# A hybrid decoder step on one core: the x tiles normed one by one, the next x and the first output stage's inputs brought forward, a sample's small work and stores moved

## The chip, the core and the metric

The kernel runs on one core of a Trainium2 chip. The metric is the device time of one execution in microseconds (us). A core has five engines with a queue of instructions each: TensorE (PE), VectorE (DVE), ScalarE (ACT), GpSimd (POOL) and SyncE (SP). They run in parallel and wait for each other through semaphores; inside one engine everything runs in the order written. Transfers are issued by SP, ACT and POOL and moved by 16 shared DMA engines.

## What is computed

One layer over 2048 prompt rows and 8 x 4 sample rows of width 1024, all in float32:

```
h = rms_norm(x, g_mix_pre)
z = h @ w_in                                   # 1024 -> 2048, split into 8 groups of 256
y_a = pool_mixer(z[:256])                      # trailing means over 2, 4, 8, 16 rows
y_b = conformer_conv(z[256:768])               # GLU, 31 taps, head LayerNorm, swish
y_c, v = chunk_spatial_gating(z[768:1280])     # head LayerNorm of v, lower-triangular 128x128
y_d = short_gated_conv(z[1280:])               # 3 taps
o = concat(y_a, y_b, y_c, y_d) @ w_out
x = x + rms_norm(o, g_mix_post)
f = square(relu(rms_norm(x, g_ffn_pre) @ w_up)) @ w_down
x = x + rms_norm(f, g_ffn_post)
```

It returns the new x of both kinds of rows, the last 15, 30 and 2 rows of three mixers' inputs (the states) for prompt and samples, and the samples' normed v.

## The kernel before, in words

**Matmuls.** Each float32 operand is split into a high and a low part. `split_hi` (ACT) writes `w_hi` from a weight panel in `raw`, `split_lo` (DVE) writes `w_lo = raw - w_hi`. PE's `three` (L1695 to L1697) multiplies hi by hi, hi by lo and lo by hi. A panel is 1024 x 256 weights (1 MB). `raw`, `w_hi` and `w_lo` have two slots each, and panel j uses slot j % 2.

**Order of the work.** The 2048 rows go in four blocks b of 512. The list `order` names the panels: first the eight input panels of each block (kind "I", called GATE, PV, AV, CV, HV, BV, UV, VV), then the four output panels of block 0 (kind "O"), then for each block the panels of the feed-forward part ("U" and "D"), with the O panels of the next block between the D panels. J2 = 32 is the first O panel. Each engine's program walks this list with code of its own. What an engine does between the panels is written out by hand, so the order of the calls in the program is the order of the work.

**Before panel 0.** SP loads four x tiles of block 0 (128 rows each) and then weight panels 0 and 1. ACT's `x_stat(b)` squares and sums the four tiles and takes one square root for all four; DVE's `x_norm(b)` takes one reciprocal and scales the four tiles. PE's `transpose_x` turns a tile into columns in the banks `tr[0]` and `tr[1]`, ACT's `h_hi(n)` and DVE's `h_lo(n)` write the two parts into `act_hi` and `act_lo`. PE transposes small parameter rows and the gating weights ahead of the first x tile, and the sample rows and a bias product behind the last one, all ahead of panel 0.

**Between two blocks.** The x tiles of block b + 1 are loaded into `raw`, which only blocks 1 to 3 leave free: their split weights come from scratch in HBM. For block 1 the loads wait until `raw` is done with the last two panels of block 0. `x_stat(b + 1)` and `x_norm(b + 1)` stand inside block b; PE transposes the tiles between the four 128-row chunks of the last panel, VV, because `act_hi` and `act_lo` have one slot. DVE spreads the 31 taps of the convolution (`taps`, L1122) over block b and the start of the next.

**The sample's small work.** In block 2, after the UV panel, ACT issues 24 small stores of sample states, then squares and roots the sample's v (L820, L822), for which DVE waits inside `sample_v` (L1278), and issues one more store.

**The first output stage.** `mix_in` (POOL) loads a tile of the four mixers' results from scratch into `mixc`, and `mix_part` (ACT, then DVE) splits it. DVE's `o_copy` moves a finished bank to `o_sb`, ACT's `o_squares` sums its squares. Between the copies stand the last block's leftovers: `v_centre`, `v_sum`, `v_scale` (LayerNorm of v), `centre`, `gate`, `conv_scale`, `conv_out`. PE's `gating_of`, `mean_of` and `var_of` serve them between the panels. After the fourth panel `f_of_first` norms the rows for the feed-forward part and PE transposes them (L1921).

Of the kernel before, what the change touches and what calls it, by code (L numbers as in the profile page):

```python
# [5 lines left out]
def hybrid_trunk_step(nc, x_prompt, x_sample, state_pool, state_conv, state_short, g_mix_pre, g_mix_post,  # L6
# [71 lines left out]
    bank_of, wrote, freed = {}, [0] * NRING, [0] * NRING  # L78
# [19 lines left out]
    with ctx:  # L98
# [37 lines left out]


# [24 lines left out]
        ch_ext = sb("ch_ext", [P, 2, HS + N1], to=p1)  # L162
        b_raw = sb("b_raw", [P, 2, N1], to=p1)
        c_short = sb("c_short", [P, 2, N1], to=p1)
        a_ext = sb("a_ext", [P, 2, HP + N1], to=p1)
# [233 lines left out]
        def x_tile(n):  # L399

            r = n % NCH
            if n < NCH:
# [45 lines left out]
        def _(sp):  # L448
            for i in range(NCH):
                sp.dma_start(x_tile(i), x_prompt[0, i * P:(i + 1) * P, :]).then_inc(x_full[i], 16)  # L450
            sp.dma_start(x_smp[:, :], x_sample.rearrange("b t c -> (b t) c")).then_inc(xsmp_full, 16)
# [12 lines left out]
            for j, (kind, b, q, p) in enumerate(order):  # L464
                s = j % 2
                if j not in part_no:
# [4 lines left out]
                    sp.dma_start(raw[:, s, :, :], source(j)).then_inc(raw_full[s], 16)  # L471
                    raw_user[s] = j
                if j == NI - 1:
                    for r in range(2):
                        sp.wait_ge(lo_ready, split_no[NI - 2 + r])
                        x_in_raw(1, r)
                if kind == "I" and p == 2 and 0 < b < NB - 1:
                    for s in range(2):
                        sp.wait_ge(x_tr, 2 * NCH * (b + 1))
                        x_in_raw(b + 1, s)  # L480
                if kind == "I" and p == 4 and b == 0:
# [13 lines left out]
        def _(pool):  # L495
# [77 lines left out]
            for j in part_no:  # L573
# [13 lines left out]
                if p == 7:  # L587
                    store(b, 0, ya_done, pool_d[:, :, :])
            store(NB - 1, 3, yd_done, c_short[:, :, :])

# [3 lines left out]
            pool.wait_ge(nst_tr, 2)  # L594
            pool.wait_ge(mix_st[0], MIX_ST)
            for i in range(2):
                mix_in(0, i)
            for g, dst in ((g_mix_post, g_mix), (g_ffn_pre, g_up), (g_ffn_post, g_out)):
                pool.dma_start(dst[:, :], g[0].partition_broadcast(P)).then_inc(s_gains, 16)
            for i in range(2):  # L600
                rows_in("x", 0, i)
# [24 lines left out]
        def _(act):  # L626
# [10 lines left out]
            def x_stat(b):  # L637
                for i in range(NCH):
                    act.wait_ge(x_full[i], 16 * (b + 1))
                    act.wait_ge(x_sq, NCH * b + i)  # L640
                    if b == 1 and i == 0:
                        act.wait_ge(smp_step, 1)
                    SC.activation(junk[:, :], x_tile(NCH * b + i), ACT.Square, accum_out=xms[:, i:i + 1])\
# [1410 lines left out]
```

## Time and profile before

| | |
|---|---|
| median of 3 runs | 2289.42 us (2289.16 to 2293.85) |
| the profiled execution's own time | 2289.91 us |
| its span, first to last instruction | 2288.1 us |
| PE busy | 2147.0 us, 94% of the span |
| PE weight load busy | 1945.0 us, 85% |
| DVE busy | 1081.4 us, 47% |
| ACT busy | 752.6 us, 33% |
| mean granted TensorE clock | 0.977 |

The clock is a share of 2.4 GHz; it has two levels, 0.5 (1.2 GHz) and 1.0. In a timeline row the bracket at the end holds the time that the engine stood idle just before, and who ended it. Times in rows count from the start of the span.

### The profile page before, as it was taken

The numbers are of one execution on the slowest core, as the hardware profiler recorded it, in microseconds if no ns is written. First come the engines' busy times: TensorE is split into PE (matmuls) and PEld (weight loads), VectorE is DVE, ScalarE is ACT, GpSimd is POOL, SyncE is SP. The second block draws the span as 40 slices with busy tenths as digits, with TensorE's granted clock in tenths as the row PEclk, the third lists the DMA queues.
The fourth block names the chain that finished last, engine by engine and source line by source line (L and its number), as shares of the span: only waits on it lengthen the run. The fifth ranks groups of instructions, "written<-read, shape, count | busy, mean of one in ns | idle before, by whom it ended". The sixth has DMA issues, their size and how long they took to land.

```text
span 2288.1 us, 32980 instructions
## 1 busy us (share of the span) xinstructions
PE 2147.0 (94%) x14425; PEld 1945.0 (85%) x14425; DVE 1081.4 (47%) x1388; ACT 752.6 (33%) x1145; POOL 115.0 (5%) x205
## 2 busy tenths in 40 slices
PE   6989997979699999999999999999999989999996
PEld 4877775768488988988898899889898989999996
DVE  3677766775643333465333346533334553334243
ACT  4233232224333223443323244332324442313131
POOL 2000110010000000000000000000000000000000
PEclk9999998989799999999999999999999999999998
DMA  6754644553232223445233334533223434222221
GB/s 211 242 212 170 212 169 170 180 192 103 102 112 93 93 93 102 131 154 166 93 99 99 98 130 148 166 100 102 93 93 119 137 115 135 85 83 78 90 74 60
DMA packets 186084, 291.87 MB, mean 128 GB/s; under 512 B 6128, under 2 KB 162453, under 8 KB 177733
## 3 DMA queue, kind: packets, MB, share of 16 engines
q1 hardware_dynamic: 160997, 168.64, 23.2%
q0 software_dynamic: 24656, 120.96, 15.0%
q8 instruction: 114, 1.87, 0.3%
q14 instruction: 30, 0.24, 0.0%
q10 hardware_dynamic: 287, 0.16, 0.0%
HBM read 247.24 MB, written 42.80 MB: 127 GB/s over the span
## 4 chain that ended last, share of the span: by engine, by line
PE 66%; issue 18%; DVE 7%; ACT 4%; DMA 3%; ACTq 0%; POOL 0%; SPq 0%; POOLq 0%; DVEq 0%
PE mm L1695 21%; PE mm L1696 21%; PE mm L1697 21%; ACT w_hi L635 2%; DVE w_lo L1079 2%; DVE conv L1122 2%; DMA mixc<-mixT_scratch 1%; DMA x_in<-in_x_prompt 1%; PE tr L1700 1%; PE tr L1729 1%; DMA raw<-in_w_in 1%; PE tr L1921 0%; DVE o_sb L1399 0%; PE mm L1756 0%; DVE conv_s L1606 0%
## 5 line engine op out<-in xcount | busy, mean ns | idle before, releaser
L1079 DVE TENSOR_TENSOR w_lo<-raw,w_hi 128x2048 fp32r<-128x2048 f32 x152 | 348.4, 2292 | 707.1 <-ACT w_hi L635 707.1
L1695 PE MATMUL mm<-act_hi,w_hi 128*128 128x512 f32 (+1 forms) x1728 | 638.5, 369 | 9.8 <-DVE act_lo L1417 6.0
L1696 PE MATMUL mm<-act_lo,w_hi 128*128 128x512 f32 (+1 forms) x1728 | 632.6, 366 | 0.0
L1697 PE MATMUL mm<-act_hi,w_lo 128*128 128x512 f32 (+1 forms) x1728 | 630.0, 365 | 0.0
L1695 PE MATMUL mm<-w_hi,u_hi 128*128 128x256 f32 (+1 forms) x2176 | 603.3, 277 | 1.5
L1697 PE MATMUL mm<-w_hi,u_lo 128*128 128x256 f32 (+1 forms) x2176 | 601.0, 276 | 0.0
L1696 PE MATMUL mm<-w_lo,u_hi 128*128 128x256 f32 (+1 forms) x2176 | 600.9, 276 | 0.0
L635 ACT ACTIVATE w_hi<-raw 128x2048 fp32r<-128x2048 f32 x152 | 290.8, 1913 | 582.0 <-PE mm L1697 581.1
L1695 PEld LDWEIGHTS mm<-w_hi,u_hi 128*128 128x128 f32 (+1 forms) x2176 | 398.3, 183 | 4.8 <-DVE u_lo L1433 3.6
L1696 PEld LDWEIGHTS mm<-w_lo,u_hi 128*128 128x128 f32 (+1 forms) x2176 | 398.3, 183 | 1.2
L1697 PEld LDWEIGHTS mm<-w_hi,u_lo 128*128 128x128 f32 (+1 forms) x2176 | 398.3, 183 | 0.7
L1695 PEld LDWEIGHTS mm<-act_hi,w_hi 128*128 128x128 f32 x1728 | 327.4, 189 | 68.8 <-issue 13.4
L1697 PEld LDWEIGHTS mm<-act_hi,w_lo 128*128 128x128 f32 x1728 | 327.1, 189 | 56.3
L1696 PEld LDWEIGHTS mm<-act_lo,w_hi 128*128 128x128 f32 x1728 | 327.1, 189 | 55.2 <-issue 2.4
L1695 PE MATMUL mm<-w_hi,act_hi 128*128 128x256 f32 (+1 forms) x736 | 210.3, 286 | 17.7 <-DVE act_lo L1365 14.9
L1697 PE MATMUL mm<-w_hi,act_lo 128*128 128x256 f32 (+1 forms) x736 | 208.2, 283 | 0.0
L1696 PE MATMUL mm<-w_lo,act_hi 128*128 128x256 f32 (+1 forms) x736 | 208.0, 283 | 0.0
L904 ACT ACTIVATE square<-mm 128x512 f32<-128x512 f32 (+1 forms) x160 | 81.8, 511 | 262.5 <-PE mm L1697 262.5
L1122 DVE SCALAR_TENSOR_TENSOR conv<-g_ext,cst,conv 128x512 f32<-128x512 f32 x240 | 162.6, 745 | 0.7 <-ACT conv L739 0.7
L1695 PEld LDWEIGHTS mm<-w_hi,act_hi 128*128 128x128 f32 (+1 forms) x736 | 133.7, 182 | 20.2 <-issue 15.5
L1431 DVE CAST u_hi<-square 128x512 fp32r<-128x512 f32 (+1 forms) x160 | 59.9, 374 | 192.3 <-ACT square L906 192.3
L1696 PEld LDWEIGHTS mm<-w_lo,act_hi 128*128 128x128 f32 (+1 forms) x736 | 133.3, 181 | 2.2 <-issue 0.5
(238 smaller groups left out, 1350.4 us busy)
## 6 DMA issues: line engine op xcount, KB each, us to landing
raw<-in_w_ffn_up SPq DMA_DIRECT2D x64, 1024.0 KB, 5.4
raw<-in_w_ffn_down SPq DMA_DIRECT2D x64, 1024.0 KB, 5.1
w_hi<-whi_scratch POOLq DMA_DIRECT2D x24, 1024.0 KB, 5.2
w_lo<-wlo_scratch POOLq DMA_DIRECT2D x24, 1024.0 KB, 7.9
raw<-in_w_out SPq DMA_DIRECT2D x16, 1024.0 KB, 5.3
raw<-in_w_in SPq DMA_DIRECT2D x8, 1024.0 KB, 9.5
whi_scratch<-w_hi POOLq DMA_DIRECT2D x8, 1024.0 KB, 8.7
wlo_scratch<-w_lo POOLq DMA_DIRECT2D x8, 1024.0 KB, 10.7
```

The lines of the kernel that those rows point to most:

```text
L635: SC.activation(w_hi[:, s, :, :], raw[:, s, :, :], ACT.Copy).then_inc(hi_ready, 1)
L904: SC.activation(square[:, at % 2, 0:c1 - c0], mm[bank][:, 0:c1 - c0], ACT.Relu).then_inc(bank_free[bank], 1)
L1079: DVE.tensor_tensor(w_lo[:, s, :, :], raw[:, s, :, :], w_hi[:, s, :, :].bitcast(fp32), ALU.subtract)\
L1122: DVE.scalar_tensor_tensor(out=c, in0=g_ext[:, t, k:k + N1], scalar=col("conv_w", 2 * k + t), in1=c, op0=ALU.mult, op1=ALU.add).then_inc(c ...
L1431: DVE.tensor_copy(u_hi[:, k, c0:c1], square[:, at % 2, 0:c1 - c0]).then_inc(u_hi_ready, 1)
L1695: PE.matmul(out, whi, xhi, start=(k == 0), stop=False)
L1696: PE.matmul(out, whi, xlo, start=False, stop=False)
L1697: return PE.matmul(out, wlo, xhi, start=False, stop=(k == K - 1))
L1700: PE.matmul(bank[:, 0:n], headmean[:, :], src, start=True, stop=True).then_inc(done, 1)
L1729: last = PE.transpose(tr[hh][:, kk * P:(kk + 1) * P], x_tile(n)[:, k * P:(k + 1) * P], ident[:, :])
```

## The change

1. **Start.** Panel 0's weights are loaded from ACT's queue as its first instruction, and panel 1's from SP ahead of the small rows. One square root on a one-column tile `warm` stands before the first x. `x_stat` and `x_norm` take one tile at a time (one root and one reciprocal each) and are interleaved with `h_hi`, `h_lo` and the split of panel 0. PE's small transposes and the bias product become `small_parts`, called after the first half of panel 0.
2. **Next x.** The four x tiles of block 1 go to `v_n` and to three tiles of `x0`, loaded from j = 3 on. Their `x_stat` stands after `split_hi(5)`. The tiles of block 2 go to `raw` without waiting for the transposes of block 1.
3. **Sample's v and small stores.** `sample_v` is cut into three parts that stand between taps at the start of block 2; the 25 sample stores and the 3 prompt state stores are issued by SP.
4. **First output stage.** The last block's state transposes (`last_rows`) stand after the first half of UV. `split_lo(J2)` stands three taps later, the first `mix_part` six taps later; `v_centre` and what follows it come behind all four `mix_part`. `mix_in(0, 0)` no longer waits for the last store of the pool mixer. `gating_of`, `mean_of` and `var_of` come one panel later.
5. **Ring.** The first output stage uses four PSUM banks, the rest six in turn.

```diff
-            bank = len(bank_of) % NRING
+            bank = turn % 4 if j < J2 + NP else (turn - 2 * NP + 4) % NRING
...
-            if n < NCH:
+            if n == NCH:
+                return v_n[:, :, :].rearrange("p a c -> p (a c)")
+            if n < 2 * NCH:
                 return x0[:, r, :]
...
+            sp.dma_start(raw[:, 1, :, :], source(1)).then_inc(raw_full[1], 16)
...
+                if j == 3:
+                    sp.wait_ge(bias_ready, 1)
+                    for r in range(NCH):
+                        sp.wait_ge(x_tr, 2 * NCH)
+                        sp.dma_start(x_tile(NCH + r), x_prompt[0, N1 + r * P:N1 + (r + 1) * P, :])\
+                          .then_inc(x_full[r], 16)
...
+            act.dma_start(raw[:, 0, :, :], source(0)).then_inc(raw_full[0], 16)
             act.wait_ge(pool_init, 5)
+            SC.activation(warm[:, :], eps[:, :], ACT.Sqrt)
...
             b = NB - 1
-            v_centre(b)
-            for i in range(2):
-                mix_part(0, i)
-            split_lo(J2 + 1)
-            v_sum(b)
-            for i in range(2, NCH):
-                mix_part(0, i)
-            v_scale(b)
-            token_panel(J2, o_copy)
+            mix_part(0, 0)
+            mix_part(0, 1)
+            taps(b, range(28, 30))
+            mix_part(0, 2)
+            taps(b, range(30, 31))
+            mix_part(0, 3)
+            split_lo(J2 + 1)
+            v_centre(b)
+            v_sum(b)
+            token_panel(J2, o_copy)
+            v_scale(b)
+            token_panel(J2 + 1, o_copy)
             centre(b)
             gate(b)
-            token_panel(J2 + 1, o_copy)
-            conv_scale(b)
             token_panel(J2 + 2, o_copy)
+            conv_scale(b)
             conv_out(b)
             last_o_panel(J2 + 3)
```

ACT in the same stage:

```diff
-            v_square(b)
-            for i in range(2):
+            for i in range(NCH):
                 mix_part(0, i)
             split_hi(J2 + 1)
-            for i in range(2, NCH):
-                mix_part(0, i)
+            v_square(b)
             v_root(b)
             token_panel(J2, o_squares)
+            token_panel(J2 + 1, o_squares)
             conv_square(b)
-            token_panel(J2 + 1, o_squares)
             conv_root(b)
             token_panel(J2 + 2, o_squares)
```

How the instructions stand on an engine, before and now:

ACT at the very start, before:

```order
L643 ACT_TABLE_LOAD
L643 ACTIVATE junk,xms<-x 128x1024 x4
L647 ACT_TABLE_LOAD
L647 ACTIVATE xroot<-xms,eps 128x4
L699 ACTIVATE cst<-tr 128x78
L701 ACTIVATE sgu_wT<-tr 128x512
L635 ACTIVATE w_hi<-raw 128x2048
L706 ACTIVATE junk,sms<-x_smp 32x1024
L708 ACTIVATE sms<-sms,eps 32x1
L653 ACTIVATE act_hi<-tr 128x4x128 x8
```

ACT at the very start, now (as far as the second tile's high part):

```order
L730 DMA raw<-in_w_in 128x8x256
L732 ACT_TABLE_LOAD
L732 ACTIVATE warm<-eps 128x1
L675 ACTIVATE junk,xms<-x 128x1024
L679 ACTIVATE xroot<-xms,eps 128x1
L675 ACTIVATE junk,xms<-x 128x1024
L679 ACTIVATE xroot<-xms,eps 128x1
L686 ACTIVATE act_hi<-tr 128x4x128 x2
L675 ACTIVATE junk,xms<-x 128x1024
L679 ACTIVATE xroot<-xms,eps 128x1
L666 ACTIVATE w_hi<-raw 128x2048
L686 ACTIVATE act_hi<-tr 128x4x128 x2
```

The one table load between the squares and the root is gone, the high part of the first tile stands ahead of the split of panel 0's weights, and the third tile's statistics stand between them.

DVE where the first output stage begins, before (the taps are `conv<-g_ext,cst,conv`, two instructions each):

```order
L1079 TENSOR_TENSOR w_lo<-raw,w_hi 128x2048
L1122 SCALAR_TENSOR_TENSOR conv<-g_ext,cst,conv 128x512 x24
L1135 TENSOR_REDUCE v_small<-v_raw 128x16
L1137 TENSOR_SCALAR v_small<-v_small 128x16
L1140 TENSOR_TENSOR v_n<-v_raw,v_small 128x1024
L1365 TENSOR_TENSOR act_lo<-mixc,act_hi 128x8x128 x2
L1079 TENSOR_TENSOR w_lo<-raw,w_hi 128x2048
```

DVE at the same place, now:

```order
L1155 SCALAR_TENSOR_TENSOR conv<-g_ext,cst,conv 128x512 x6
L1111 TENSOR_TENSOR w_lo<-raw,w_hi 128x2048
L1155 SCALAR_TENSOR_TENSOR conv<-g_ext,cst,conv 128x512 x12
L1416 TENSOR_TENSOR act_lo<-mixc,act_hi 128x8x128 x2
L1155 SCALAR_TENSOR_TENSOR conv<-g_ext,cst,conv 128x512 x4
L1416 TENSOR_TENSOR act_lo<-mixc,act_hi 128x8x128
L1155 SCALAR_TENSOR_TENSOR conv<-g_ext,cst,conv 128x512 x2
L1416 TENSOR_TENSOR act_lo<-mixc,act_hi 128x8x128
L1111 TENSOR_TENSOR w_lo<-raw,w_hi 128x2048
L1168 TENSOR_REDUCE v_small<-v_raw 128x16
```

Twelve taps' instructions and `v_centre` stood between the weights and the first `mix_part` and no longer do.

DVE at the end of the first output stage, before (from the copies of the second panel to those of the fourth):

```order
L1378 COPY o_sb<-mm 128x2x256
L1165 RECIPROCAL inv_c<-inv_c 128x512 x2
L1168 TENSOR_TENSOR conv<-conv,inv_c 128x512 x2
L1378 COPY o_sb<-mm 128x2x256
L1079 TENSOR_TENSOR w_lo<-raw,w_hi 128x2048
L1378 COPY o_sb<-mm 128x2x256
L1174 TENSOR_TENSOR conv<-sqcv,inv_c 128x512 x2
L1378 COPY o_sb<-mm 128x2x256 x2
```

DVE at the same place, now (from `gate` to the copies of the fourth panel):

```order
L1219 TENSOR_TENSOR u_sb<-v_raw,u_sb 128x512 x2
L1429 COPY o_sb<-mm 128x2x256
L1111 TENSOR_TENSOR w_lo<-raw,w_hi 128x2048
L1429 COPY o_sb<-mm 128x2x256
L1198 RECIPROCAL inv_c<-inv_c 128x512 x2
L1201 TENSOR_TENSOR conv<-conv,inv_c 128x512 x2
L1207 TENSOR_TENSOR conv<-sqcv,inv_c 128x512 x2
L1429 COPY o_sb<-mm 128x2x256 x2
```

The reciprocals stood ahead of the third panel's copies and its weight split, and now stand behind them, directly ahead of `conv_out`.

## Rows read from the trace of the kernel before

**Rows 1.** The page's first part: busy time of each engine.

```profile
PE 2147.0 (94%) x14425; PEld 1945.0 (85%) x14425; DVE 1081.4 (47%) x1388; ACT 752.6 (33%) x1145; POOL 115.0 (5%) x205
```

**Rows 2.** Waits of PE: who waited for whom, us in total, times, longest.

```profile
PE tr L1729 <- DVE act_lo L1111: 29.2, 6, 14.0
PE tr L1921 <- DVE f_sb L1409: 20.9, 5, 15.6
```

**Rows 3.** Timeline of the start: start us, us, engine, instruction, [idle before].

```profile
12.04 1.06 ACT L643 ACTIVATE junk<-x 128x1024 bf16<-128x1024 f32 x1 [1.73 <-DMA x<-in_x_prompt]
13.21 1.28 ACT L647 ACT_TABLE_LOAD   x1
...
18.36 1.91 ACT L635 ACTIVATE w_hi<-raw 128x2048 fp32r<-128x2048 f32 x1 [0.93 <-DMA raw<-in_w_in]
...
31.14 0.69 DVE L1111 TENSOR_TENSOR act_lo<-tr,act_hi 128x512 fp32r<-128x512 f32 x1 [0.16 <-ACT act_hi L653]
...
33.13 0.80 PE L1695 MATMUL mm<-act_hi,w_hi 128*128 128x512 f32 x1
...
46.80 0.28 PE L1695 MATMUL mm<-w_hi,act_hi 128*32 128x256 f32 x1
```

**Rows 4.** Timeline at the end of block 0, DVE and PE.

```profile
135.46 0.18 DVE L1099 RECIPROCAL xinv<-xroot 128x4 f32<-128x4 f32 x1 [5.84 <-ACT xroot L647]
135.67 4.88 DVE L1104 SCALAR_TENSOR_TENSOR raw<-raw,xinv,gpre 128x1024 f32<-128x1024 f32 x4
...
151.77 1.94 PE L1729 MATMUL tr<-ident,raw 128*128 128x128 f32 x8 [6.94 <-DVE act_lo L1111]
```

**Rows 5.** Timeline at the end of block 2, DVE and PE.

```profile
354.48 0.41 DVE L1275 TENSOR_TENSOR vs_n<-zs,vs_small 32x256 f32<-32x256 f32 x1
...
372.44 0.41 DVE L1278 TENSOR_REDUCE vs_small<-vs_out 32x4 f32<-32x256 f32 x1 [17.54 <-ACT vs_out L820]
...
386.78 1.94 PE L1729 MATMUL tr<-ident,raw 128*128 128x128 f32 x8 [14.00 <-DVE act_lo L1111]
```

**Rows 6.** Windows, PE alone: us, busy (instructions), granted clock, DMA share, GB/s.

```profile
151.80:157.70 5.90, 5.90 (x28) 0.50 0.00 0
386.80:391.90 5.10, 5.10 (x32) 0.69 0.01 3
545.20:567.50 22.30, 22.30 (x192) 1.00 0.28 85
```

**Rows 7.** Timeline where the first output stage begins.

```profile
489.23 2.29 DVE L1079 TENSOR_TENSOR w_lo<-raw,w_hi 128x2048 fp32r<-128x2048 f32 x1 [10.53 <-ACT w_hi L635]
491.44 15.98 DVE L1122 SCALAR_TENSOR_TENSOR conv<-g_ext,cst,conv 128x512 f32<-128x512 f32 x24
507.35 1.21 DVE L1135 TENSOR_REDUCE v_small<-v_raw 128x16 f32<-128x1024 f32 x1
...
513.46 0.55 PE L1695 MATMUL mm<-w_hi,act_hi 128*128 128x256 f32 x1 [14.87 <-DVE act_lo L1365]
...
519.14 1.06 ACT L855 ACTIVATE act_hi<-mixc 128x1024 fp32r<-128x1024 f32 x1 [4.33 <-DMA mixc<-mixT_scratch]
...
527.68 2.57 PE L1756 MATMUL mm<-sgu_wT,v_n 128*64 128x128 f32 x32
...
531.60 0.68 PE L1695 MATMUL mm<-w_hi,act_hi 128*128 128x256 f32 x1
```

**Rows 8.** Timeline where the first output stage ends.

```profile
545.44 2.29 DVE L1079 TENSOR_TENSOR w_lo<-raw,w_hi 128x2048 fp32r<-128x2048 f32 x1 [6.91 <-ACT w_hi L635]
...
550.03 6.57 DVE L1165 RECIPROCAL inv_c<-inv_c 128x512 f32<-128x512 f32 x2 [1.70 <-ACT inv_c L685]
...
568.09 0.69 DVE L1174 TENSOR_TENSOR conv<-sqcv,inv_c 128x512 f32<-128x512 f32 x1 [3.94 <-ACT inv_c L693]
...
570.11 1.28 DVE L1378 COPY o_sb<-mm 128x512 f32<-128x512 f32 x2
...
583.11 1.97 PE L1921 MATMUL tr<-ident,f_sb 128*128 128x128 f32 x8 [15.58 <-DVE f_sb L1409]
```

More of the change, by code:

```diff
@@ L702, in _ @@
               .then_inc(init_copied, 1)
-            split_hi(0)
-            act.wait_ge(xsmp_full, 16)
-            act.wait_ge(x_sq, NCH)
-            SC.activation(junk[0:NS, :], x_smp[:, :], ACT.Square, accum_out=sms[:, 0:1]).then_inc(smp_step, 1)
-            act.wait_ge(smp_step, 1)
-            SC.activation(sms[:, 1:2], sms[:, 0:1], ACT.Sqrt, bias=eps[0:NS, :], scale=1.0 / D).then_inc(smp_step, 1)
-            for n in range(NCH):
-                h_hi(n)
-            split_hi(1)
             act.wait_ge(smp_tr, 1)
@@ L758, in _ @@
                     split_hi(5)
+                    for i in range(NCH):
+                        x_stat(NCH + i)
                 if b == 1:
@@ L1289, in _ @@
             x_norm(0)
+            x_norm(1)
+            h_lo(0)
+            x_norm(2)
             split_lo(0)
-            for n in range(NCH):
-                if n == 1:
-                    dve.wait_ge(smp_step, 2)
-                    DVE.reciprocal(sms[:, 2:3], sms[:, 1:2]).then_inc(smp_step, 1)
-                    dve.wait_ge(smp_step, 3)
-                    DVE.scalar_tensor_tensor(out=x_smp[:, :], in0=x_smp[:, :], scalar=sms[:, 2:3], in1=gpre[0:NS, :],
-                                             op0=ALU.mult, op1=ALU.mult).then_inc(smp_step, 1)
-                h_lo(n)
+            h_lo(1)
+            x_norm(3)
+            h_lo(2)
+            h_lo(3)
+            dve.wait_ge(smp_step, 2)
+            DVE.reciprocal(sms[:, 2:3], sms[:, 1:2]).then_inc(smp_step, 1)
+            dve.wait_ge(smp_step, 3)
+            DVE.scalar_tensor_tensor(out=x_smp[:, :], in0=x_smp[:, :], scalar=sms[:, 2:3], in1=gpre[0:NS, :],
+                                     op0=ALU.mult, op1=ALU.mult).then_inc(smp_step, 1)
+            split_lo(1)
             dve.wait_ge(smp_hi, 1)
@@ L1301, in _ @@
                               act_hi[:, :, N1:NX].bitcast(fp32), ALU.subtract).then_inc(smp_lo, 1)
-            split_lo(1)
             dve.wait_ge(init_tr, 3)
@@ L1345, in _ @@
                 if b < NB - 1:
-                    x_norm(b + 1)
-                if b == 2:
-                    sample_v()
+                    for i in range(NCH):
+                        x_norm(NCH * (b + 1) + i)
                 taps(b, range(15, 19))
@@ L1351, in _ @@
                 if last:
+                    taps(b, range(19, 22))
                     split_lo(J2)
-                    taps(b, range(19, 31))
+                    taps(b, range(22, 28))
                 else:
@@ L1708, in _ @@
             pe.wait_ge(pool_init, 8)
-            pe.wait_ge(s_rows, 16 * len(ROWS))
-            PE.transpose(tr[0][:, 0:NROW], rows[:, :], ident[0:NROW, 0:NROW]).then_inc(init_tr, 1)
-            pe.wait_ge(pool_init, 9)
-            for h in range(4):
-                last = PE.transpose(tr[1][:, h * P:(h + 1) * P], sgu_w_sb[:, h, :], ident[:, :])
-            last.then_inc(init_tr, 1)
             def transpose_x(n, hh):
```

243 lines of the change are left out of this document (144 added, 99 removed).

## The prediction

> **What bounds the kernel now.** I read the page's busy times first. The reader sees PE busy for 94% of the span and DVE for 47% [rows 1]: the time is PE's work plus the 6% in which PE stands, so an edit that removes no matmul can only win in PE's gaps. Then the waits of PE: the longest sums are transposes that wait for DVE's low part of x (29.2 us in 6 waits, the longest 14.0) and transposes that wait for DVE's normed rows (20.9 us, the longest 15.6) [rows 2]. Then the timeline at each gap. There are five that the change touches: the start, until 33.13 us [rows 3]; 6.94 us at the end of block 0 [rows 4]; 14.00 us at the end of block 2 [rows 5]; 14.87 us ahead of the first output panel [rows 7]; and 15.58 us behind the fourth [rows 8]. Behind 590 us the change moves nothing but the bank numbers, so I expect the rest of the program to shift as a whole.
>
> A gap costs more than itself. After the 6.94 us PE ran 28 matmuls in 5.9 us at a granted clock of 0.50 (1.2 GHz), against 192 matmuls in 22.3 us at 1.00 (2.4 GHz), 0.116 us each [rows 6]. The 28 are of several shapes; the cadence of the same shape is twice as slow, so I charge 0.46 us for each us that PE is busy at 1.2 GHz.
>
> **Start.** Before, the last x tile landed at about 12.0 us, the root waited for all four, a table load of 1.28 us stood ahead of it, and then the first weight split (18.36 to 20.27) stood ahead of the first `h_hi` [rows 3]. Now each tile goes through by itself. Tile 3's x: the 1 MB of panel 0's weights, which landed by 18.36, is requested beside the x tiles. Bound below: x is not delayed, and the last tile lands at 12.0. Bound above: all of that 1 MB goes ahead of it; before, it landed 18.36 - 12.04 = 6.3 us behind the last x tile [rows 3], with other transfers in between: 18.3. I take the middle, 15.0, since both queues are full at once and the same bytes have to land. Then statistics with root 1.5, reciprocal and scaling 1.5, PE's eight transposes 2.0, and high and low parts: with DVE's weight split (2.3 us) ahead of the second tile's low part, tile 1 is done near 20.6, tile 2 near 23.5 and tile 3 near 26.2 us. First matmul: 26.2 instead of 33.13. The small transposes, the sample rows and the bias product are not gone: they stand inside panel 0 and now cost 2.8 us there (0.4 + 1.0 + 1.0 + 1.1 at 1.2 GHz, partly at the higher clock; they wait for two short ACT copies, which are free by then). Panel 0 took 33.13 to 46.80 = 13.67 us [rows 3], and ends now at 26.2 + 13.7 + 2.8 = 42.7. **Gain 4.1 us**, between -1 and 6.
>
> On the table load: the row shows 1.28 us, with the root starting as soon as it ends, 14.50 us [rows 3]. [...]
>
> **End of block 0.** DVE was through its taps at 129.6 and stood 5.84 us for the root of block 1's x, since the loads had waited for `raw` [rows 4]. Now these tiles land some 70 us earlier and ACT handles them after panel 3, when it has nothing due. DVE goes on at once. Four reciprocals instead of one add 3 x 0.2 us and their hand-over: 0.8 us. So `h_lo` comes 5.06 us earlier against PE; the gap of 6.94 becomes 1.9. Without the long gap the 5.9 us at 1.2 GHz go too: 5.9 x 0.46 = 2.7 us. A short gap can still bring one shorter fall; I charge 0.75 us. **Gain 7.0 us** (5 to 9). The new waits here (ACT's taps of block 1 and `v_square` for the transposes of all four tiles; SP's x loads for the bias, ahead of panel 4's weights) end more than 20 us before anyone needs what is queued behind them.
>
> **End of block 2.** DVE finished the first half of `sample_v` at 354.9 and stood 17.54 us until ACT, which had issued 24 stores first, gave it the squares at 372.4 [rows 5]. Everything behind it (14 taps, `short_out`) was 20 us late, and PE waited 14.00 us for `h_lo`. With the sample work between taps at the start of the block, where DVE otherwise stands for the first panels, that wait is zero: `h_lo` would be ready at about 366, and is then bound by the transposes themselves. The 25 stores go to SP's queue, which has nothing else due in block 2. The fall of the clock after the gap (0.69 over 5.1 us [rows 6], so 3.2 us at the lower level) goes as well: 3.2 x 0.46 = 1.4. **Gain 15.4 us** (13 to 16.5).
>
> **Start of the output stage.** PE is ready at 513.46 - 14.87 = 498.6. DVE had 24 tap instructions of 0.67 us and then `v_centre` ahead of the first `mix_part` [rows 7]. Now six of them fill the 10.53 us that DVE stood before the weight split, and twelve follow it: 491.4 + 8.1 = 499.5. ACT's copy of v ends at 499.3, its high part at 500.3, DVE's low part at 501.5. PE starts at 501.6 instead of 513.46: the gap is 3.0 instead of 14.87.
>
> But the next waits come up. Tile 2's data is loaded when tile 0's is split; before, this took from 513.3 to its low part at 521.4 (ACT's part began at 519.14 after a wait for the DMA [rows 7]), 8.2 us. From 501.5 that is 509.7, while PE is through two tiles at 507.3: 2.5 us. Panel 0 of the stage ends at 515.5, panel 1 at 527.0, at 11.5 us a panel (22.3 us for two [rows 6], with their ends). `v_centre` to `v_scale` now stand behind all four `mix_part`, the split of the second panel and half of the copies: 514.6 + 2.7 + 1.1 + 1.2, then on ACT a root with table load 1.6, squares 1.1 and split 1.9, then on DVE split 2.3, copy 0.7, and 1.5: 529.0. PE waits 2.1 us, does gating and mean in 3.9 us (527.68 to 531.60 [rows 7]) and ends the third panel at T = 533.0 + 11.5 = 544.5.
>
> **End of the output stage.** This is where the change gives back. Var follows the third panel, T + 0.9. ACT's roots stand ahead of its work on the third panel, so the split of the fifth weight panel waits for them, and DVE's second copy waits for the split: roots to T + 2.7, squares 3.8, `split_hi` 5.7, `split_lo` 8.0, copy 8.7. Only then come the two reciprocals, 6.57 us [rows 8], and the product: T + 16.0; swish with a table load 2.9; `conv_out` T + 19 and 20.4; the copies of the fourth panel start at T + 21.0. From there to the first transpose the rows show 583.11 - 570.11 = 13.0 us [rows 8], which nothing shortens. So the transposes begin at T + 34.0 = 578.5, though PE is done with the fourth panel at 557.4: the 15.58 us gap grows to 21. From 583.11 to 578.5: **gain 4.6 us** for the whole stage (-1 to 9), out of 11.9 won at its head.
>
> **Sum.** 4.1 + 7.0 + 15.4 + 4.6 = 31.1 us, from the profiled execution's own 2289.9 us: 2258.8. The median of the runs is 0.5 us lower, so I say 2258.5. The bank order (four, then six) costs nothing: in this stage a bank is refilled two panels later, and the copies are 5 us ahead of that. The state transposes move by half a panel without changing, and ACT's waiting for them between the two halves of UV (about 1 us) lies beside PE's work.
>
> **Rivals.**
> (a) *The start gives nothing.* The x tiles get a share only, ACT stands behind the weight split, and the small parts stall inside panel 0. Every step 3 us later (29.2) and 4.9 instead of 2.8 us in the panel: 47.8, a loss of 1.0. Total 26.0, time 2263.5. For it: weights and x have landed back to back, so the transfers are already dense [rows 3]. Against: only the last tile is critical. [...] Chance 0.13.
> (b) *The end of the stage is not DVE's.* If the reciprocals slip beside PE's fourth panel as before, the gap stays 15.6 and the stage gains 10.0: 2253. Against: the order on DVE, written out. Chance 0.08.
> (c) *Block 0's end does not move*: the early x of block 1 is late through a wait that I hold harmless, and the 7.0 us stay: 2265.5. Chance 0.08.
> (d) *Slower.* The new pattern of four short gaps and one of 21 us keeps the clock at 1.2 GHz through the stage and into the feed-forward part. At 0.46 us per busy us, the 31.1 us are eaten by 68 us of busy time at the lower level, and from 78 us on the kernel is slower by over 0.2%; with all 100 us behind 501 us it would be 2304. Against: before, the clock came back within 6 us of work after each gap [rows 6]. Chance 0.03.
> The forecast itself has 0.66; 0.02 is left for a result within 0.2% by several misses at once.
>
> **How the numbers follow.** The forecast's own bounds add to about +-5 us (the terms are independent), 2253.5 to 2263.5. The range takes in (a), (b) and (c): 2251 to 2268. About 0.2%, 4.6 us, is what a measurement of this kernel can tell from no change. Every case but (d) and the rest is faster by more: 0.95, 0.02, 0.03.
>
> **What would show it.** First matmul of panel 0 near 26 us; PE's wait at the end of block 0 near 2 us and none over 2 us at the end of block 2; the first output matmul 3 us behind the last of VV; waits of about 2 us for tile 2 and for gating; DVE idle for some 10 us before the split of the fifth weight panel, and a wait near 21 us ahead of the first feed-forward transposes. The prediction is wrong if the first matmul is behind 29 us, if that last wait is under 16 us, or if a PE wait over 3 us stands where none is named here.

## The result, and the profile after

| | before | after |
|---|---|---|
| median | 2290.74 us (2289.16 to 2293.85, 4 runs) | 2275.16 us (2271.18 to 2279.85, 4 runs) |
| profiled execution, own time / span | 2289.91 / 2288.1 us | 2279.85 / 2278.0 us |

The ratio is 0.9931, 95% interval 0.9909 to 0.9954. The kernel is faster, but by 15.6 us and not by the 31.1 us of the sum, and 2275.16 lies outside the range of 2251 to 2268. The profiled execution of the change is the slowest of its four, so the two traces are 10.1 us apart and not 15.6: what is read from this pair holds a few us that the medians don't. The first part of the page after, for [rows 1]:

```profile
PE 2169.0 (95%) x14425; PEld 1964.6 (86%) x14425; DVE 1083.2 (48%) x1400; ACT 755.1 (33%) x1157; POOL 115.7 (5%) x205
```

PE has the same 14425 instructions and 22 us more busy time (2169.0 against 2147.0). Less waiting was forecast, more work was not.

**The gaps.** Waits of PE, for [rows 2]: the longest wait for `act_lo` falls from 14.0 to 4.7 us (that one stands at the start, between two x tiles' transposes), the one for `f_sb` grows from 15.6 to 20.2.

```profile
PE tr L1977 <- DVE f_sb L1460: 24.5, 5, 20.2
...
PE tr L1774 <- DVE act_lo L1144: 9.9, 5, 4.7
```

Timeline rows of the change (start, us, engine, instruction, [idle before]), for [rows 3, 4, 5, 7, 8] in this order:

```profile
9.85 1.06 ACT L675 ACTIVATE junk<-x 128x1024 bf16<-128x1024 f32 x1 [3.25 <-DMA x<-in_x_prompt]
...
15.81 1.91 ACT L666 ACTIVATE w_hi<-raw 128x2048 fp32r<-128x2048 f32 x1 [0.29 <-DMA raw<-in_w_in]
...
26.83 0.76 PE L1748 MATMUL mm<-act_hi,w_hi 128*128 128x512 f32 x1 [1.50 <-DVE act_lo L1144]
...
42.63 0.28 PE L1748 MATMUL mm<-w_hi,act_hi 128*32 128x256 f32 x1
...
142.28 1.23 PE L1774 MATMUL tr<-ident,x 128*128 128x128 f32 x8 [1.61 <-DVE act_lo L1144]
...
367.57 1.22 PE L1774 MATMUL tr<-ident,raw 128*128 128x128 f32 x8 [1.20 <-DVE act_lo L1144]
370.69 0.76 PE L1748 MATMUL mm<-act_hi,w_hi 128*128 128x512 f32 x1 [1.89 <-DVE act_lo L1144]
...
476.50 0.55 PE L1748 MATMUL mm<-w_hi,act_hi 128*128 128x256 f32 x1 [3.06 <-DVE act_lo L1416]
...
502.11 2.57 PE L1808 MATMUL mm<-sgu_wT,v_n 128*64 128x128 f32 x32 [0.16 <-DVE v_n L1186]
...
523.03 2.29 DVE L1111 TENSOR_TENSOR w_lo<-raw,w_hi 128x2048 fp32r<-128x2048 f32 x1 [10.09 <-ACT w_hi L666]
...
525.84 6.56 DVE L1198 RECIPROCAL inv_c<-inv_c 128x512 f32<-128x512 f32 x2
...
550.96 0.90 PE L1977 MATMUL tr<-ident,f_sb 128*128 128x128 f32 x3 [20.22 <-DVE f_sb L1460]
```

Each is near its forecast: first matmul 26.83 (26.2), the sample matmuls of panel 0 at 42.63 (42.7), 1.61 us at the end of block 0 (1.9), nothing over 2 at the end of block 2, 3.06 us ahead of the output stage (3.0), DVE idle 10.09 us (10), the last wait 20.22 (21). The first feed-forward matmul starts at 569.92, before at 602.15: **32.2 us ahead**, and the sum said 31.1. The time is lost behind this point. The lead in the two traces, read at the first U matmul of a group, is 26.0 us at 785, 21.4 at 1426, 17.3 at 1854 and 12.2 at 2164 us of before.

**Where it goes.** Windows, PE alone (us, busy, clock, DMA share, GB/s). The first row of each kernel runs from near the first feed-forward transpose to some 10 us behind the clock's return (1.00 from 605.10 on in before, from 574.80 on in the change), the second to the next U group, the third is one undisturbed pass over one U and one D group. Before:

```profile
581.60:615.70 34.10, 21.34 (x93) 0.66 0.23 82
615.70:696.40 80.70, 78.32 (x537) 1.00 0.34 106
696.46:785.26 88.80, 88.67 (x578) 1.00 0.30 95
```

After:

```profile
544.60:585.50 40.90, 23.36 (x97) 0.63 0.29 103
585.50:669.20 83.70, 81.31 (x533) 0.96 0.33 103
669.28:759.27 89.99, 89.92 (x579) 1.00 0.29 94
```

The third row decides: the same work, full clock, no wait, and 89.99 instead of 88.80 us. The page's groups show which matmuls. Before:

```profile
L1695 PE MATMUL mm<-w_hi,u_hi 128*128 128x256 f32 x2048 | 568.0, 277 | 1.5
```

After:

```profile
L1748 PE MATMUL mm<-w_hi,u_hi 128*128 128x256 f32 x2048 | 573.6, 280 | 0.8
```

Each D matmul (256 columns of weights against a chunk of `u_hi` or `u_lo` as the stationary operand) takes 280 instead of 277 ns. With the short forms there are 3 x 2176 = 6528 of them; their busy time goes from 1805.2 to 1825.4 us. From start to start, the 384 D matmuls of the pass take 45.2 us (714.09 to 759.27) instead of 44.0 (741.27 to 785.26): 0.1177 against 0.1145 us each, the changes of panel included. The 192 U matmuls ahead of them take 44.8 us in both.

The rest is the clock: from 669.28 on the lead is 27.2, so 5.05 us went in the first pass, of which 1.2 are the D matmuls. The other 3.9 us lie beside a longer time at the lower level (granted clock 0.63 over 40.9 us, then 0.96, against 0.66 over 34.1, then 1.00). In that pass PE is busy at 0.50 for 4.9 us up to 574.80 and for 6.3 us from 608.90 to 615.70, against 3.0 us up to 605.10 in before.

**Theory A: the place of `u_hi` and `u_lo` sets the pace of the D matmuls.** The diff has one line that I had priced at nothing: `warm = sb("warm", [P, 1])`, four bytes in each of the 128 partitions, allocated behind `act_lo`. The traces hold no addresses; those given here stand in the programs built from the runs' `kernel.py`. There `u_hi` begins at byte 169920 of the partition in before and at 169952 in the change, `u_lo` at 187328 and at 187360. "Even" and "odd" below are short for a start at an even multiple of 32 bytes (a multiple of 64) or at an odd one: before, both were even, now both are odd. That these 32 bytes matter is at this point an estimate, from nothing but the 89.99 beside 88.80 us; e1 and e3 measure it. Rivals: the bank order, which also changes only behind the stage; something else in the changed order. (The diff also allocates `ch_ext` behind `c_short`, which the list of changes leaves out; e1 keeps that.)

### The profile page after: what moved, and what is told of

Same layout as the page of the kernel before. It is cut to its first block, busy times and chain, and to the rows that moved or that the text cites. A ratio compares the mean times of both kernels' runs of the same rounds, so it can differ in the third digit from the quotient of the medians.

```text
span 2278.0 us, 33025 instructions
## 1 busy us (share of the span) xinstructions
PE 2169.0 (95%) x14425; PEld 1964.6 (86%) x14425; DVE 1083.2 (48%) x1400; ACT 755.1 (33%) x1157; POOL 115.7 (5%) x205
## 3 DMA queue, kind: packets, MB, share of 16 engines
q0 software_dynamic: 24656, 120.96, 15.1%
## 4 chain that ended last, share of the span: by engine, by line
PE 68%; issue 19%; DVE 6%; ACT 4%; DMA 3%; POOL 0%; POOLq 0%; ACTq 0%; DVEq 0%
PE mm L1748 22%; PE mm L1749 22%; PE mm L1750 22%; ACT w_hi L666 2%; DVE w_lo L1111 2%; DMA mixc<-mixT_scratch 1%; DMA x_in<-in_x_prompt 1%; PE tr L1753 1%; DVE conv L1155 1%; DMA raw<-in_w_in 1%; PE tr L1977 0%; PE mm L1808 0%; DVE o_sb L1450 0%; PE tr L1774 0%; DVE conv_s L1659 0%
## 5 line engine op out<-in xcount | busy, mean ns | idle before, releaser
L1750 PE MATMUL mm<-w_hi,u_lo 128*128 128x256 f32 (+1 forms) x2176 | 608.6, 280 | 0.0
L1749 PE MATMUL mm<-w_lo,u_hi 128*128 128x256 f32 (+1 forms) x2176 | 607.5, 279 | 0.0
```

Of the source, the lines that this page charges most:

```text
L1749: PE.matmul(out, whi, xlo, start=False, stop=False)
L1750: return PE.matmul(out, wlo, xhi, start=False, stop=(k == K - 1))
```

## The experiments

All ratios are against the kernel before, measured beside each experiment on the same chip. Its median there lay between 2289.46 and 2293.85 us, so experiments that were measured apart are better compared by their ratios and traces than by their medians.

**e1: the change without its tile.** The early root writes into `yroot`, which nobody uses then.

```diff
-        warm = sb("warm", [P, 1])
...
-            SC.activation(warm[:, :], eps[:, :], ACT.Sqrt)
+            SC.activation(yroot[:, 0:1], eps[:, :], ACT.Sqrt)
```

> The changed kernel without the four-byte tile `warm` (the early square root writes into a column of `yroot`), so that every tile behind it lies 32 bytes lower, where it lay before the change. Theory A (the place of u_hi and u_lo in SBUF sets the pace of the D panels' matmuls): their start-to-start time returns from 0.1179 to 0.1147 us, the 6528 of them take about 20 us less, and the kernel about 2255 us. Theory B (the new order of the PSUM banks): no change, about 2275 us. Theory C (a state of that one execution): no change beyond its scatter.

Measured 2255.96 us (2252.12 to 2260.33), ratio 0.985 (0.9833 to 0.9867). The same pass:

```profile
667.20:756.00 88.80, 88.67 (x579) 1.00 0.30 95
```

It is back at 88.80 us, and 33.6 us are won against the 2289.56 of before, near the 31.1 of the sum. The order of the instructions is the change's (last wait 20.20 us).

**e2: the change with another phase of the six-bank ring.**

```diff
-            bank = turn % 4 if j < J2 + NP else (turn - 2 * NP + 4) % NRING
+            bank = turn % 4 if j < J2 + NP else (turn - 2 * NP + 2) % NRING
```

> The changed kernel with the feed-forward part's banks counted on from bank 2, as before the change, and everything else as changed. Theory B (the bank order): D matmuls back to 0.1147 us, the kernel about 2255 us. Theory A (the place in SBUF): 0.1179 us as in the changed kernel, about 2275 us.

Measured 2276.37 us (2273.92 to 2279.62), ratio 0.994 (0.9925 to 0.9954): as the change. The banks are not it.

```profile
664.59:754.59 90.00, 89.93 (x579) 1.00 0.29 94
```

**e3: the kernel before plus an unused tile.**

```diff
         act_lo = sb("act_lo", [P, K, NX], f32r)
+        pad = sb("pad", [P, 1])
```

> The kernel before, with an unused four-byte tile allocated where the changed kernel has `warm`, and nothing else. Theory A: the D matmuls go from 0.1147 to about 0.1179 us and the kernel loses about 20 us, to 2310. Theory B and C: no difference from the kernel before, 2290.

Measured 2307.03 us (2305.75 to 2310.93), ratio 1.0075 (1.006 to 1.009). Four bytes that nothing reads or writes cost 17.5 us (by the interval 14 to 21):

```profile
696.80:786.79 89.99, 89.92 (x578) 1.00 0.30 94
```

e1 and e3 together settle the cause: tile off, 33.6 us won; tile alone, 17.5 lost; 33.6 - 17.5 = 16.1, and the change measured 15.6.

**e4: e1 with `act_hi` and `act_lo` moved by 32 bytes too.** They stood at an odd multiple, before and after (`act_hi` at byte 77152, `act_lo` at 94560; in e4 77120 and 94528). The trace of before held the hint, in the same shape. Forty-eight matmuls of an O panel (stationary from `act_hi`) lie between these two rows of its timeline, 0.1167 us each:

```profile
953.26 0.28 PE L1696 MATMUL mm<-w_lo,act_hi 128*128 128x256 f32 x1
...
958.86 0.28 PE L1696 MATMUL mm<-w_lo,act_hi 128*128 128x256 f32 x1
```

and forty-eight of a D panel (stationary from `u_hi` or `u_lo`, even in this kernel) between these, 0.1133 each:

```profile
1078.31 0.28 PE L1697 MATMUL mm<-w_hi,u_lo 128*128 128x256 f32 x1
...
1083.75 0.28 PE L1697 MATMUL mm<-w_hi,u_lo 128*128 128x256 f32 x1
```

```diff
-        eps = sb("eps", [P, 1])
         sgu_wT = sb("sgu_wT", [P, 4, P])
...
         act_lo = sb("act_lo", [P, K, NX], f32r)
+        eps = sb("eps", [P, 1])
```

> As the run without the `warm` tile, and the four-byte tile `eps` allocated behind act_lo instead of ahead of it, which moves act_hi and act_lo down by 32 bytes to a multiple of 64 and leaves u_hi and u_lo at one. Theory A, in the form that a stationary operand at an odd multiple of 32 bytes costs 3.2 ns a matmul: the O panels' matmuls go from 0.117 to 0.1147 us (1536 of them, -3.5 us or so; in the I panels the VV ones too), and the input and up panels may or may not go faster, since there act is the moving operand; about 2250 us. If only a moving operand's place mattered, the D panels could not have changed, since theirs (w_hi, w_lo) has not moved.

Measured 2242.28 us (2240.43 to 2243.17), ratio 0.9787 (0.9771 to 0.9803), 13.7 us below e1 and below both kernels:

```profile
661.27:749.42 88.15, 88.02 (x579) 1.00 0.30 96
```

The pass is 0.65 us shorter than e1's. Its 192 U matmuls, where `act_hi` and `act_lo` are the moving operand, go at 0.2300 instead of 0.2334 us from start to start; that was left open in the forecast, and with it the time falls below the 2250. The O matmuls go at 0.1133 instead of 0.1167 (forty-eight between these two rows):

```profile
905.92 0.28 PE L1749 MATMUL mm<-w_hi,act_lo 128*128 128x256 f32 x1
...
911.36 0.28 PE L1749 MATMUL mm<-w_hi,act_lo 128*128 128x256 f32 x1
```

The same forty-eight D matmuls take 5.60 us in the change (1072.61 to 1078.21), 0.1167 each: in these three traces O and D panels have the same two cadences, 0.1133 where the operand is even and 0.1167 where it is odd. The up matmuls of 272 columns in the last block stay at 0.1257.

**e5: only `u_lo` odd.**

```diff
         u_hi = sb("u_hi", [P, K, NX], f32r, to=p2)
+        gap = sb("gap", [P, 1], to=p2)
         u_lo = sb("u_lo", [P, K, NX], f32r, to=p2)
```

> This is e1 (the change without its 4-byte tile) plus an unused 4-byte tile between u_hi and u_lo: u_hi begins at an even multiple of 32 bytes as in e1, u_lo and what lies behind it at an odd one. Theory A (a stationary operand at an odd multiple of 32 bytes makes each D matmul that loads it some 3 ns longer): only the third of the D matmuls whose stationary is u_lo is longer, 608 us of busy time against 601 for that line's x2176 group, the other two stay at 601 to 603; the time is about 2256.0 + 6.5 = 2262.5 us. Rival B (it is the place of something else behind u_lo, for example an operand that PE doesn't read): all three groups are longer, about 2273 to 2276 us. Rival C (only the first of the two matters, or the two tiles' distance): no group is longer, 2256 us.

Measured 2280.7 us (2279.9 to 2287.74), ratio 0.9954 (0.9938 to 0.9971). **Theory A in its simple form falls**, and the time lies above rival B's range too: one odd operand costs more than two (the pass takes 90.56 us, with both odd 89.99). All three kinds of D matmul are slow:

```profile
L1748 PE MATMUL mm<-w_hi,u_hi 128*128 128x256 f32 (+1 forms) x2176 | 613.4, 282 | 0.6
L1750 PE MATMUL mm<-w_hi,u_lo 128*128 128x256 f32 (+1 forms) x2176 | 611.7, 281 | 0.0
L1749 PE MATMUL mm<-w_lo,u_hi 128*128 128x256 f32 (+1 forms) x2176 | 610.2, 280 | 0.0
```

Either one odd operand slows the whole trio, or a tile behind `u_lo` counts, since these moved too. The next two kernels tell it apart.

**e10: e1 with the unused tile behind `u_lo`.**

```diff
         u_lo = sb("u_lo", [P, K, NX], f32r, to=p2)
+        gap = sb("gap", [P, 1], to=p2)
         square = sb("square", [P, 2, N1], to=p2)
```

> This is e1 (the change without its 4-byte tile) with an unused 4-byte tile behind u_lo: u_hi and u_lo stay at an even multiple of 32 bytes, only square and f2_sb behind them move to an odd one. In e5, where u_hi was even and u_lo odd, all three kinds of D matmul were slow, not only the one that loads u_lo, so two explanations are left. A2 (one odd stationary in the trio of matmuls slows all three): here nothing is slow, 0.985 of before, 2256 us, D groups at 601 to 603 us of busy time. B (what counts is a tile behind u_lo, written by DVE and ACT while PE works): the D groups are slow as in e5, at 608 to 615 us, 0.9925 to 0.9955 of before.

Measured 2258.93 us (2254.52 to 2260.32), ratio 0.9858 (0.9842 to 0.9875), e1's within the intervals. What lies behind doesn't count:

```profile
668.20:757.00 88.80, 88.67 (x579) 1.00 0.29 95
```

**e11: only `u_hi` odd**, `u_lo` at e1's address.

```diff
-        ysum = sb("ysum", [P, NCH + 1])
...
-        yinv = sb("yinv", [P, NCH + 1])
...
+        yinv = sb("yinv", [P, NCH + 1], to=p2)
         u_hi = sb("u_hi", [P, K, NX], f32r, to=p2)
+        ysum = sb("ysum", [P, NCH + 1], to=p2)
         u_lo = sb("u_lo", [P, K, NX], f32r, to=p2)
```

> This is e1 with two 20-byte tiles (yinv, ysum) put ahead of u_hi and between u_hi and u_lo: u_hi is at an odd multiple of 32 bytes, u_lo exactly where it is in e1, and everything behind it too. A2 (one odd stationary in the trio slows all three, whichever it is): the D groups are slow, 608 us or above against 601 to 603, ratio to before 0.9925 to 0.9955. B (what counts lies behind u_lo) or A3 (only u_lo counts): nothing is slow, 0.985, 2256 us. The plain theory A, that each matmul pays for its own stationary, would give two thirds of e1's distance to the change: 0.990; e5 has spoken against it.

Measured 2284.74 us (2281.98 to 2289.99, 10 runs), ratio 0.9975 (0.9965 to 0.9985), 29 us above e1:

```profile
663.35:754.11 90.76, 90.71 (x578) 1.00 0.29 93
```

The pass takes 88.80 us with both even (e1), 89.99 with both odd (the change), 90.56 with only `u_lo` odd (e5) and 90.76 with only `u_hi` odd (e11; it begins at byte 169888 there). B and A3 fall, and A2 holds in both mixtures: the three kinds of D matmul are slowed together (282, 281 and 281 ns in e5, 284, 281 and 280 in e11, against 277, 276 and 276 in e1). Its size was forecast too small: the ratio lies above A2's 0.9925 to 0.9955, because the mixture is worst. Why, no run here shows. In both mixtures `u_lo` lies 17440 bytes behind `u_hi` and in all others 17408, a multiple of 64, so "one odd" and "a distance that is no multiple of 64" are the same thing here.

**e8: the first weights back on SP's queue.** What was the load from ACT's queue worth?

```diff
+            sp.dma_start(raw[:, 0, :, :], source(0)).then_inc(raw_full[0], 16)
             sp.dma_start(raw[:, 1, :, :], source(1)).then_inc(raw_full[1], 16)
...
-            act.dma_start(raw[:, 0, :, :], source(0)).then_inc(raw_full[0], 16)
```

> This is e1 with the load of the first weight panel back on SP's queue, behind the four x tiles. It asks what the load from ACT's queue is worth at the start. My theory (the requests from both queues interleave, so weights come earlier and x a little later): here the last x tile lands 2 to 4 us earlier and the weights 1 to 3 us later, near 18 us; the first matmul waits for the weights' split and starts within 1 us of e1's (26.8), time 2256 +- 2 us. Rival (a) of the prediction (the load from ACT's queue costs the start what it should bring): the first matmul starts 2 to 3 us earlier than in e1, near 24, time 2253.5 us. Opposite rival (the weights on ACT's queue carry the gain at the start): the first matmul starts 3 us or more later, 2259 us or above.

Measured 2257.59 us (2254.57 to 2258.81), ratio 0.9842 (0.9826 to 0.9859), e1's. Timeline of e8, start:

```profile
5.95 1.04 ACT L675 ACTIVATE junk<-x 128x1024 bf16<-128x1024 f32 x1
...
16.14 1.91 ACT L666 ACTIVATE w_hi<-raw 128x2048 fp32r<-128x2048 f32 x1 [1.89 <-DMA raw<-in_w_in]
...
27.16 0.77 PE L1747 MATMUL mm<-act_hi,w_hi 128*128 128x512 f32 x1 [1.50 <-DVE act_lo L1143]
```

Against e1, from which it differs by this load alone, the second x tile's squares start 3.6 us earlier (5.95 against 9.56), the weights' split 0.2 us later (16.14 against 15.92; 1 to 3 were forecast), and the first matmul 0.2 us later (27.16 against 26.94). When the last x tile landed can't be read, since its squares stand behind the split. So with the weights' load on ACT's queue the second x tile came at least 3.6 us later (in e1 ACT waits 3.47 us for it, in e8 it doesn't wait), and the weights' split started 0.2 us earlier. The second queue is not what gives the start its gain. Which other part of the new start does (the tiles one by one, the early table load, the small parts inside panel 0), no run separates.

The traces do show what the start now waits for. The first matmul comes 11.02 us behind the start of the weights' split in all three: 15.81 and 26.83 in the change, 15.92 and 26.94 in e1, 16.14 and 27.16 in e8, each time with the split waiting for the transfer of the weights. So in these three runs the landing of the weights and the chain behind it set the start, and x does not.

**e9: before with part 3 alone** (the sample's v between the taps, its stores on SP).

```diff
-                    taps(b - 1, range(25, 27))
+                    taps(b - 1, range(25, 26))
+                    if b == 2:
+                        sample_v_centre()
+                    taps(b - 1, range(26, 27))
```

and so on for `sample_v_sum`, `sample_v_scale` and ACT's two instructions.

> This is the kernel before with part 3 of the change alone: sample_v in three pieces between the taps at the start of block 2, its 25 stores on SP. No new tile, the ring and everything else as before. The prediction's step: the wait of 14.0 us at the end of block 2 goes, and the fall of the clock behind it, 15.4 us together: 2289.6 - 15.4 = 2274.2 us. Rival 1 (DVE's pieces only move the wait into the start of block 2, where PE then waits for the low part or a bank): 2282 to 2290 us. Rival 2 (the wait goes but the clock behind it doesn't change): 2275.6 us, with a granted clock near 0.69 in the 5 us from the first transpose on.

Measured 2273.85 us (2272.98 to 2276.24), ratio 0.9919 (0.9905 to 0.9934). Timeline of e9, end of block 2:

```profile
377.83 1.23 PE L1744 MATMUL tr<-ident,raw 128*128 128x128 f32 x8 [1.20 <-DVE act_lo L1114]
...
380.94 0.47 PE L1710 MATMUL mm<-act_hi,w_hi 128*128 128x512 f32 x1 [1.89 <-DVE act_lo L1114]
```

The 14.00 us are gone. The first matmul of block 3 starts at 380.94 instead of 397.35; 0.7 us of that lead existed before block 2, so the part gives 15.7 us there (forecast 15.4). The time fits the forecast of 2274.2 better than it should: the kernel before took 2293.85 us beside this run and not 2289.6, and the ratio makes the gain 18.6 us, with an interval of 15.1 to 21.8.

**e6: e4 with DVE's reciprocals earlier**, for the 20 us that the change leaves at the end of the stage.

```diff
-            token_panel(J2 + 2, o_copy)
+            o_copy(J2 + 2, 0)
             conv_scale(b)
+            split_lo(J2 + 4)
+            o_copy(J2 + 2, 1)
```

On ACT `split_hi(J2 + 4)` stands ahead of the swish and of the second half's squares.

> This is e4 (the change without its 4-byte tile, both act tiles moved to an even multiple of 32 bytes) with the order at the end of the first output stage changed: on ACT conv_root directly behind the first half of the third panel's squares, the swish behind the split of the fifth weight panel; on DVE the reciprocals and the product (conv_scale) behind the first copy of the third panel, ahead of the weight split and the second copy. Theory (DVE's reciprocals standing idle-free some 6 us earlier is what ends the 20.2 us wait ahead of the first feed-forward transposes): the wait falls to about 14 us, the time from 2242.3 to about 2236.3 us. Rival 1 (then the copies of the fourth panel or the f rows' scaling end the wait, at nearly the same time): wait 18 us or more, 2240 to 2242 us. Rival 2 (the second copy of the third panel now comes so late that PE waits for its bank in the fifth panel): a new wait of PE of 2 us or more ahead of it, time as before or worse.

Measured 2235.84 us (2234.55 to 2237.23), ratio 0.9767 (0.9753 to 0.978). Timeline of e6:

```profile
513.24 6.57 DVE L1199 RECIPROCAL inv_c<-inv_c 128x512 f32<-128x512 f32 x2 [6.31 <-ACT inv_c L718]
...
538.36 1.97 PE L1980 MATMUL tr<-ident,f_sb 128*128 128x128 f32 x8 [14.14 <-DVE f_sb L1461]
```

The wait is 14.14 us, against 20.5 in e4, and the median 6.4 us below e4's, as expected. The intervals of the two ratios overlap, so the wait is the firmer evidence. The chain from the reciprocals to the transposes did set the end of the stage.

**e7: e6 with the sixth weight panel's split behind the first feed-forward tile.**

```diff
-                for i in range(3):
+                x2_stat(0, 0)
+                split_hi(J2 + 5)
+                for i in range(1, 3):
```

DVE's `split_lo(J2 + 5)` stands behind its first `f_tile`.

> This is e6 with the split of the sixth weight panel moved behind the first tile of the feed-forward inputs, on ACT and on DVE. Theory (DVE's 2.3 us and ACT's 1.9 us split stand ahead of the first f tile and so on the path that ends the wait): the wait ahead of the first feed-forward transposes is another 1.8 to 2.3 us shorter than in e6, time about 2234.5 us. Rival (the split was in the shadow of ACT's roots; moved, it makes PE wait at the next weight panel): no shorter wait, or a new wait for w_lo or w_hi, 2236 us or above.

Measured **2233.08 us** (2230.33 to 2235.57, 5 runs), ratio 0.9752 (0.9739 to 0.9765), against 2289.46 of before. The fastest kernel of the study.

```profile
536.04 1.97 PE L1985 MATMUL tr<-ident,f_sb 128*128 128x128 f32 x8 [12.36 <-DVE f_sb L1464]
```

The wait is 1.78 us shorter than in e6. The medians differ by 2.8 us, but the two intervals overlap, so the gain rests on the trace more than on the times.

## Why the prediction was wrong

**The step that failed** is in the first paragraph: "Behind 590 us the change moves nothing but the bank numbers, so I expect the rest of the program to shift as a whole." The change also moves every tile behind `act_lo` by 32 bytes, `u_hi` and `u_lo` among them. I had read the new tile as a means to bring the table load forward and asked only what its instruction costs. The sum has no term for it. Measured on its own (e3) the term is -17.5 us, and e1 without it lies 33.6 us below before. None of the signs of being wrong that the prediction names looks at PE's pace behind 590 us. The mechanism is of no rival either: (d) lets the clock eat the gain, and the clock in the long pass is 1.00.

The terms, as leads between the two traces (the last one is read at PE's last matmul, where 10.65 us of lead are left):

| step | forecast | shown |
|---|---|---|
| start (46.80 to 42.63) | 4.1 | 4.2 |
| end of block 0 (lead then 12.1) | 7.0 | 7.9 |
| first 7 us of block 2 (lead then 11.0) | 0 | -1.1 |
| end of block 2 (397.35 to 370.69, lead then 26.7) | 15.4 | 15.7 |
| first 7 us of block 3 (lead then 25.2) | 0 | -1.5 |
| output stage (lead then 32.2) | 4.6 | 7.1 |
| feed-forward part | 0 | -21.6 in the profiled pair, 3.9 of it clock |

- **Start: the sum was right, in part by luck.** I took 15.0 us for the last x tile's landing and made it critical. In the trace the third tile's squares run at 14.05 without waiting for data, and the last tile stands behind ACT's weight split, at 18.58. The weights' landing and the 11.02 us chain behind it set the first matmul (e8). Rival (a) is refuted: it had the first matmul at 29.2. That the x tiles get only a share beside the weights is borne out by e8 (the second tile's squares start at 5.95 there and at 9.56 in e1), but x is not what is waited for. On the table load the trace agrees with the row: 1.28 us at 1.30, and the root behind it starts 0.27 us after its end, when POOL's constants are there.
- **End of block 0**: a wait of 1.61 us, and no fall of the clock behind it:

```profile
142.30:148.20 5.90, 4.92 (x40) 1.00 0.00 0
```

 I had charged 0.75 us for a shorter fall, an estimate; that is most of the 0.9 us by which the term was too small. Rival (c) is refuted.
- **End of block 2** was right, and e9 shows the same 15.7 us by itself. What the sum has no term for is the clock behind the short gaps at the starts of blocks 2 and 3: in the change PE's clock stays at its lower level longer there. PE in the first 7 us of block 3, before and after:

```profile
397.35:404.35 7.00, 7.00 (x25) 0.80 1.06 371
```

```profile
370.69:377.69 7.00, 7.00 (x18) 0.56 1.07 375
```

 That is 1.5 us of the lead. At the start of block 2 it is 0.76 against 0.58 in the same 7 us, and 1.1 us.
- **Output stage**: the head gave 11.8 us (14.87 to 3.06), forecast 11.9. The two small waits behind it did not come: none for tile 2, 0.16 us for gating instead of 2.1 (the chain that gave 529.0 adds up to 528.7, which changes little). The state transposes cost nothing, as forecast: the lead is 0.6 us smaller in the second half of UV and back at 25.2 when PE is ready for the output stage. At the end 4.8 us were given back (lead 37.0 at the first output matmul, 32.15 at the first feed-forward transpose), forecast 7.3. So the stage gave 2.5 us too much, and the clock at the starts of blocks 2 and 3 took 2.6 us that the sum didn't have: the lead of 32.2 beside a sum of 31.1 is in part luck. Rival (b) is refuted: the wait is 20.22 us, and e6 shows that the order on DVE sets it.
- **The charge of 0.46 us**: behind the 6.94 us gap of before, at a granted share of 0.50, the 18 starts from 153.72 to 157.56 us are 0.2133 us apart (256 columns, stationary from `act_hi`); at 1.00 that shape goes at 0.1167. That is 1.83 times and not twice as slow, and 1 - 0.1167 / 0.2133 = 0.45, so the charge stands. The traces give the clock only as a share, 0.5 or 1.0, with values between as means over a window. The GHz of the text ahead stand as an estimate from these times: 256 columns in 0.2133 us are 1.2 columns per ns, taken as 1.2 GHz at a share of 0.50, and 2.4 GHz is its double. At 1.00 the same columns in 0.1167 or 0.1133 us are 2.2 or 2.3 per ns, not 2.4.
- **Clock**: 3.9 us more of rival (d)'s kind appear in the profiled execution, behind the longer wait. They are no fixed cost: for the first pass the change took 99.4 us at a granted clock of 0.94 and e1 98.2 at 0.94, but e2, with the same order, 95.6 at 0.98 (568.97 to 664.59), and before 94.3 at 0.98. What decides between them, no run shows. Nor did the clock come back within 6 us of work behind every gap of before, as the argument against (d) has it: behind the 15.58 us gap of [rows 8] it is 0.50 from 583.11 to 605.10, with PE busy for 10.74 us.

## What to carry to other kernels

A new tile can move the operands allocated behind it: here four bytes moved `u_hi` and `u_lo` by 32 and cost 17.5 us (e3), and four bytes behind `u_lo` cost nothing that the times show (e10, ratio 0.9858 beside e1's 0.985). List the start addresses of the matmul operands before and after, however small the tile, and put new small tiles last. Where two groups of matmuls of one shape run at different cadence at full clock, compare the addresses of their operands; here that difference (0.1167 against 0.1133 us) stood in the trace of before, and moving the two slow operands was worth 13.7 us. A forecast that says "the rest shifts as a whole" needs a sign of its own: the time of one pass of the rest, before and after. A gap that closes at its head shows what sets its tail: the order on the engine that comes next (here DVE's reciprocals) is the next thing to move.

## What the runs showed of the hardware that was not expected

- **Moving an operand's tile by 32 bytes changed the pace of the matmuls that read it.** Times are from start to start within a panel, at a granted clock of 1.00. Matmuls of 256 columns: 0.1133 us with the stationary operand even (D in before, `u_hi` at byte 169920; O in e4, `act_hi` at 77120), 0.1167 with it odd (D in the change, 169952; O in before, 77152). The U matmuls of 512 columns, where `act_hi` and `act_lo` are the moving operand: 0.2300 with them even (e4), 0.2334 odd (e1). The U matmuls of 272 columns stay at 0.1257 when `act_hi` and `act_lo` move (e4). That the parity decides is the reading that fits these places; with both operands moved, 32 bytes was the only distance measured.
- **With one of `u_hi` and `u_lo` odd the pass was slower than with both.** 88.80 us (both even, e1), 89.99 (both odd, the change), 90.56 (e5) and 90.76 (e11) with one odd. The matmuls that load the even operand are slower as well (282 and 281 ns in e5 for those with `u_hi`, 277 and 276 in e1).
- What PE does with such an address, and why the mixture costs most, stays open; a run with the three matmuls of a trio in another order was not tried. Every even start of `u_hi`, `u_lo`, `act_hi` and `act_lo` here lay 64 bytes behind a multiple of 128, so whether a multiple of 128 does better was not tried either.
